# Six convolution taps move ahead of the softplus steps, and the chunk state updates move behind the softplus sums, in two mixers of a fused two-block kernel

## The reference, cut to what matters

```
proj = h @ w_in                      # (256, 1024) @ (1024, 7184)
sb_q, sb_k, sb_v, conv_in, gla_q, gla_k, gla_v, gla_r, gla_lr, gate_logits = split(proj)

# branch 0, stick-breaking attention, 8 heads of 64
z = q k^T / 8
log_keep  = where(earlier, log_sigmoid(-z), 0)
log_stick = reverse_cumsum(log_keep) - log_keep
w = where(earlier, exp(log_sigmoid(z) + log_stick), 0);  out = w v

# branch 1, depthwise causal convolution, 31 taps on 512 channels
u = a * sigmoid(g);  y = conv31(u) + conv_b;  layer norm over channels;  silu

# branch 2, gated linear attention, 4 chunks of 64 tokens
log_alpha = log_sigmoid(lr @ w_alpha + b_alpha) / 16
S_n = diag(prod alpha) S_{n-1} + sum_s (k_s * decay_to_end_s) v_s^T;   o = q S_n
o = rms_norm(o) * silu(r)

merged = sum_g sigmoid(gate_g) * (branch_g @ w_branch_g);   return merged @ w_out
```

## Time and profile before

| | |
|---|---|
| median of 3 runs | 1984.97 us (1984.62 to 1986.65) |
| profiled execution, its own time | 1984.6 us |
| its span, first to last instruction | 1982.8 us |
| PE busy | 1949.4 us (98%) |
| DVE busy | 1376.0 us (69%) |
| ACT busy | 1153.0 us (58%) |
| POOL busy | 79.0 us (4%) |
| mean granted PE clock | 0.999 of full |
| first mixer, sq product to w_out | about 990 to 1170 us of the span |
| second mixer | the same rows 608.0 us later |

### The profile page before, as it was taken

How to read it: one execution, slowest core, us unless ns; L and a number is a source line. 1 busy time by engine, 2 the same in 40 slices (tenths; PEclk the granted TensorE clock), 3 DMA queues, 4 the chain that set the end, 5 groups by cost and what they waited for, 6 DMA issues and landing times.

```text
span 1982.8 us, 27313 instructions
## 1 busy us (share of the span) xinstructions
PE 1949.4 (98%) x10594; PEld 1654.4 (83%) x10594; DVE 1376.0 (69%) x2239; ACT 1153.0 (58%) x1801; POOL 79.0 (4%) x147
## 2 busy tenths in 40 slices
PE   7999999999999999999999999999999999999998
PEld 5998899987878888888997788888888897778887
DVE  4457676666876766765698897655766587987763
ACT  4345465445665556664646757755765646666752
POOL 0000000001100000000100000000000100000000
PEclk9999999999999999999999999999999999999999
DMA  9797755666367977875543468765967534368871
GB/s 340 252 310 252 259 176 185 202 244 205 128 217 223 284 211 219 234 213 203 195 140 125 149 213 237 220 207 165 254 210 226 192 123 160 123 198 250 222 216 42
DMA packets 340256, 407.64 MB, mean 206 GB/s; under 512 B 67740, under 2 KB 234076, under 8 KB 340128
## 3 DMA queue, kind: packets, MB, share of 16 engines
q1 hardware_dynamic: 335696, 394.04, 63.0%
q0 software_dynamic: 3456, 9.37, 1.5%
q10 hardware_dynamic: 976, 2.49, 0.4%
HBM read 390.40 MB, written 1.05 MB: 197 GB/s over the span
## 4 chain that ended last, share of the span: by engine, by line
PE 85%; DVE 8%; ACT 5%; issue 1%; DMA 1%; POOL 0%; SPq 0%; DVEq 0%; POOLq 0%; ACTq 0%
PE bank L969 23%; PE bank L1005 20%; PE bank L1007 20%; PE bank L1006 20%; DVE junk L2964 2%; DVE wlo L2243 1%; DVE wlo L2232 1%; PE bank L1054 1%; ACT whi L1593 1%; ACT whi L1583 1%; DMA raw<-in_w_mod 1%; ACT gate L2165 1%; DVE tm L3123 0%; ACT junk L1648 0%; ACT full L1659 0%
## 5 line engine op out<-in xcount | busy, mean ns | idle before, releaser
L2232 DVE TENSOR_TENSOR wlo<-raw,whi 128x1024 fp32r<-128x1024 f32 x358 | 431.0, 1224 | 238.4 <-ACT whi L1583 233.7
L1583 ACT ACTIVATE whi<-raw 128x1024 fp32r<-128x1024 f32 x360 | 372.3, 1052 | 300.1 <-PE bank L1007 144.2
L1005 PE MATMUL bank<-whi,xTh 128*128 128x512 f32 (+1 forms) x1344 | 525.7, 391 | 2.8 <-DVE xTl L2306 2.6
L1007 PE MATMUL bank<-whi,xTl 128*128 128x512 f32 (+1 forms) x1344 | 520.5, 387 | 0.0
L1006 PE MATMUL bank<-wlo,xTh 128*128 128x512 f32 (+1 forms) x1344 | 520.2, 387 | 0.0
L2243 DVE SCALAR_TENSOR_TENSOR wlo<-raw,cols,whi 128x512 fp32r<-128x512 f32 (+1 forms) x592 | 403.0, 739 | 126.0 <-ACT whi L1593 125.6
L1593 ACT ACTIVATE whi<-raw,cols 128x512 fp32r<-128x512 f32 (+1 forms) x592 | 376.5, 702 | 81.2 <-PE bank L1007 45.9
L1005 PEld LDWEIGHTS bank<-whi,xTh 128*128 128x128 f32 x1344 | 252.6, 188 | 57.0 <-DVE xTl L2306 3.4
L1007 PEld LDWEIGHTS bank<-whi,xTl 128*128 128x128 f32 x1344 | 252.5, 188 | 51.7
L1006 PEld LDWEIGHTS bank<-wlo,xTh 128*128 128x128 f32 x1344 | 252.7, 188 | 50.0 <-issue 0.5
L969 PE MATMUL bank<-xTh,whi 128*128 128x256 f32 x696 | 197.1, 285 | 0.0
(11 more groups left out here) (382 smaller groups left out, 2482.8 us busy)
## 6 DMA issues: line engine op xcount, KB each, us to landing
raw<-in_w_in SPq DMA_DIRECT2D x68, 1024.0 KB, 5.1
raw<-in_ffn_w_in SPq DMA_DIRECT2D x132, 512.0 KB, 5.6
raw<-in_ffn_w_gate SPq DMA_DIRECT2D x88, 512.0 KB, 3.9
raw<-in_ffn_w_up SPq DMA_DIRECT2D x88, 512.0 KB, 5.1
raw<-in_ffn_w_down SPq DMA_DIRECT2D x40, 1024.0 KB, 5.1
raw<-in_w_mod SPq DMA_DIRECT2D x36, 1024.0 KB, 5.6
raw<-in_ffn_w_out SPq DMA_DIRECT2D x30, 1024.0 KB, 6.4
raw<-in_w_out SPq DMA_DIRECT2D x12, 1024.0 KB, 5.1
```

The lines of the kernel that those rows point to most:

```text
L1005: e.matmul(o, hi[:, kc, sl], wh[:, c], start=at == 0 and k == 0, stop=False)
L1007: ins = e.matmul(o, lo[:, kc, sl], wh[:, c], start=False, stop=fin)
L1583: e.activation(wh, raw, ACT.Copy).then_inc(m.whi_done, 1)
L2232: e.tensor_tensor(wl, raw, wh.bitcast(F32), ALU.subtract).then_inc(m.wlo_done, 1)
```

## The change

All of it is in `Vector.mixer`. Two taps are hung on steps 2 and 3 of gvr, one on each step of gr, and two follow gr; the tuple of the softplus steps gives out 8 taps where it gave 14: one instead of two in steps 1 to 5, and one instead of two in step 9. Chunks 0 and 1 are called in step 6 and chunks 2 and 3 in step 7 as before, but behind that step's `spl` and no longer ahead of it. The number of instructions of each kind stays the same on every engine, and the lists of the other engines stay as they are.

```diff
@@ Vector.mixer
         self.stream(2)
-        self.stream(4)
+        self.stream(4, between={2: tap, 3: tap})
         for i in range(2):
             bank, _ = self.filled("gvr", l, i)
             e.tensor_copy(m.gv[:, i, 256:512], bank[:, 0:256]).then_inc(m.gv_done, 1)
-        self.stream(2)
+        self.stream(2, each=tap)
+        several(2)
         step = [0]
...
         def each():
             n = step[0]
             step[0] += 1
-            several((0, 2, 2, 2, 2, 2, 0, 0, 2, 2, 0, 0)[n])
+            several((0, 1, 1, 1, 1, 1, 0, 0, 2, 1, 0, 0)[n])
             if 2 <= n < 10:
                 values(n - 2)
             if n < 8:
                 scores(n)
+            if n in (6, 7):
+                chunks(2 * n - 12, 2 * n - 11)
...
-        self.stream(4, between={2: lambda: chunks(0, 1), 3: lambda: chunks(2, 3)}, each=each)
+        self.stream(4, each=each)
```

## The result

| kernel | median, us | runs | ratio to before, 95% interval |
|---|---|---|---|
| before | 1985.0 | 6 | |
| changed | 1992.08 (1991.18 to 1993.36) | 6 | 1.0035 [1.0024, 1.0045] |

The change makes the kernel 7.1 us slower. The direction was the forecast's; the sum held 4.2 us of it, and the median lies 0.6 us above the range of 1986.2 to 1991.5.

A forecast was written before the change was run, and what follows sets the result against it. TensorE, busy 98% of the span, was taken as the bound, with only its waits to win. A new wait less recovered waits plus VectorE's tail gave + 2.1 us a mixer, + 4.2 in all: 1989.1 us, range 1986.2 to 1991.5.

The forecast's parts named there:

- the sum: Per mixer + 3.80 - 1.53 - 0.81 - 0.43 + 1.08 = + 2.1 us; + 4.2 us in all.
- Step 1: Ahead of head 0: moved taps delay VectorE's `spl`, so TensorE gets a new wait of 3.8 us.
- no clock loss: TensorE behind the new wait at head 0: granted clock assumed to stay at 2.4 GHz, costing nothing.
- Step 2: Head 1: the old wait of 1.70 us goes, less 0.1 us of latency; TensorE is 2.27 us late.
- the 1.53 of the sum: Term for head 1: TensorE's lateness was to fall by 1.53 us after the new wait at head 0.
- Step 3: Heads 2 to 7: `spl` follows ScalarE's ln; 0.81 us won at head 5, 0.43 at head 7, 1.03 us late.
- Step 4: VectorE's tail behind head 7: chunks 2 and 3 make the last tap, ScalarE's square and then TensorE 2.1 us late.
- The case with the clock in it: Sticks of head 1: lateness kept, or a step at 1.2 GHz; + 7 to + 10 us in all; chance 0.10.

The follow-up runs named there:

- e3: Changed kernel without the two taps behind gr, which go back to softplus steps 2 and 3; 1983.57 us.
- e5: Changed kernel with one of the two taps behind gr put back into softplus step 2; 1987.51 us.
- e4: Changed kernel with 15 matmuls without use put ahead of the sticks of head 0 in each mixer; 1989.08 us.
- e8: Changed kernel again without an edit, in the same job as the run with 7 matmuls without use; 1991.95 us.
- e1: Kernel before with only the chunk updates moved behind the softplus sums of heads 6 and 7, all taps staying; 1990.13 us.
- e6: Kernel before with three taps moved into VectorE's idle time, one behind the gv copies and two behind gk's third fill, chunks unmoved; 1977.47 us.
- e7: Kernel before with three taps moved into VectorE's idle gaps and the chunk updates behind the sums of heads 6 and 7; 1981.58 us.
- e9: Changed kernel with 7 matmuls without use ahead of the sticks of head 0 in each mixer; 1989.88 us.

## Why the prediction was wrong

**Step 1, the new wait: right.** 3.80 us forecast, 3.63 measured (11.24 against 7.61), for the reasons given: 2.34 us for the shifted copies and three taps in a row ahead of `la`. e3 and e5 take the wait down with the taps of that row.

**The clock: wrong, and nearly the whole of the miss of 3.0 us.** The step that failed is "I take no clock loss". It stood on the earlier trace rows, a wait of 3.83 us in a window with a granted clock of 1.00. That reading does not hold. These are the matmuls of that stretch of the kernel before, 0 to 27 us, and the same ones from 100 to 200 us (durations in ns, min/median/max):

```profile
L969 PE MATMUL bank<-raw,sct x36: 1030/1061/1063, 6.9 to 26.3; 128*32 128x512 f32 x36
```

```profile
L969 PE MATMUL bank<-raw,sct x64: 592/592/617, 108.1 to 153.3; 128*32 128x512 f32 x64
```

At 1061 ns where 592 is the time at full clock, TensorE ran at the low rate around that wait, and it had done so since its first matmul at 6.9 us. The 1.00 in the column contradicts the durations in the same window, and the durations decide. A clock that was low ahead of the wait cannot show whether a wait makes it fall, so the row bore nothing out, and "no clock loss" stood without a reason. The clock's price in rows is 1.51 us at head 1 and 1.41 at the merge (e4), 2 x 1.4 = 2.8 us in both mixers (an estimate from the profiled executions), and more where the low stretch is longer (e8, first mixer: merge 4.55 us late).

**Step 2, head 1: right but for the clock.** 2.27 us late forecast, 2.10 in e4, 3.61 in the changed kernel. In e4 1.53 us were won back between heads 0 and 1, the 1.53 of the sum.

**Step 3, heads 5 and 7: right.** No wait for `spl` behind head 0 is left, and ScalarE's ln releases each sum. In e4 TensorE is 1.28 us late at head 5 and 0.84 at head 7, forecast 1.46 and 1.03.

**Step 4, the tail: right.** 2.1 us at the square and at the end forecast, 1.93 and 1.94 in e4. e1, e6 and e7 show that the square carries the mixer. One detail differs: TensorE takes the lateness over at a fill of gate4 (0.67 us at L2243), before L2232, whose wait stayed at 1.32 us where about 2.3 were forecast unless a fill took part of it.

**The sum and the range.** 4.2 us forecast; e4, which is the changed kernel without the fall of the clock, is 3.7 us above before. The changed kernel adds 3.0. The case with the clock in it, 1992 to 1995 us, had a chance of 0.10 together with another mechanism, and the range stopped at 1991.5. The measured 1992.08 lies in that case, by its clock mechanism; it priced a whole step at the low rate, 2.7 us, which is what e8's first mixer lost at head 1 (17.79 against 15.05), and the changed kernel's first mixer lost 1.51.

Open: why the profiled execution of the changed kernel was 2.08 us late ahead of the decay matmul; 1.4 us of it is more idle time of TensorE in the first 200 us of the span. e8 is not late there (1046.63 at the decay matmul), so it is no part of the change.

## What to carry to other kernels

Idle time of an engine is worth only what fits between two rows that nobody waits for: of 8.1 us of it on VectorE, three taps fitted free (e6), four cost a wait of 0.3 us on TensorE (e3) and six one of 3.5 us. Before work is moved behind a critical result, look for what then stands behind that work: the chunk updates won 0.46 us at one wait and made the end of each mixer 2.2 us later. And a new wait on TensorE is to be priced with matmuls at the lower clock behind it: here that came behind every wait of 3.5 us, behind one of four of 1.9 us and behind none of 1.5 us. Whether a trace shows it is read off the durations of equal matmuls, not off the clock column alone.

## What the runs showed of the hardware that was not expected

Fifteen matmuls without use, put into a wait that was there anyway, made the kernel 3 us faster (1992.08 to 1989.08 us; each against before in its own job, + 7.1 and + 3.7 us), and in the profile TensorE's clock stayed at 2.4 GHz. Seven were enough in one mixer and not in the other (e9). The price is not fixed: in the first mixer, two profiled executions of one kernel (changed and e8) had head 1 at 16.56 and at 17.79 us, 1.5 and 2.7 us above the 15.05 without a fall.
